# Two more down units prepared in the last up chunk's chain, and half of the final sums added one unit earlier

## The reference

```python
def conv_ffn(h, w_up, conv_w, conv_b, w_down):          # D=2048, FFN_DIM=5632
    u = causal_dwconv(h @ w_up, conv_w, conv_b)          # width 3
    g, val = jnp.split(u, 2, axis=-1)
    return (jax.nn.silu(g) * val) @ w_down

# first block (attention and state-space mixers come before this)
    h = rms_norm(x, norm_ffn_g[l]) * (1.0 + scale_f) + shift_f
    x = x + gate_f * conv_ffn(h, w_up[l], conv_ffn_w[l], conv_ffn_b[l], w_down[l])
return rms_norm(x, final_norm_g)
# second block (RWKV and pooling mixers), with its own weights: the same form
# shift, scale, gate = silu(c) @ w_ada + b_ada, six vectors of 2048 a block
```

## Time and profile before

| | us |
|---|---|
| median of 3 runs | 2575.4 |
| runs | 2571.93, 2575.4, 2576.75 |
| profiled execution, own time | 2577.9 |
| its span, first to last instruction | 2576.2 |
| PE busy | 2395.2 (93%) |
| DVE busy | 1948.6 (76%) |
| ACT busy | 1176.8 (46%) |
| DMA | 615.76 MB, mean 239 GB/s |
| granted TensorE clock, mean | 0.967 |

### The profile page before, as it was taken

One profiled execution on the slowest core, in us unless ns is written; L12 is line 12 of the kernel. 1 busy time (PEld: TensorE's weight loads), 2 busy tenths in 40 slices (PEclk: granted clock), 3 DMA queues, 4 the chain that ended last, 5 costly groups with the idle time before them and its releaser, 6 DMA issues.

```text
span 2576.2 us, 42584 instructions
## 1 busy us (share of the span) xinstructions
PE 2395.2 (93%) x17274; PEld 2148.4 (83%) x17274; DVE 1948.6 (76%) x2310; ACT 1176.8 (46%) x1290; POOL 96.1 (4%) x184
## 2 busy tenths in 40 slices
PE   4899958899999999999899889999899999999997
PEld 4899838888888888887699788889788888888886
DVE  6988878888797788878788576668888655566655
ACT  3344364355553345543444344434565543455442
POOL 0020000000000000000000000000000000000000
PEclk8999979999999999999999999889999999999999
DMA  8988956767777887768578122218576545555552
GB/s 358 421 332 323 341 182 252 303 259 279 280 298 298 330 304 275 272 260 341 189 270 318 67 89 97 95 58 305 227 279 258 187 172 193 183 185 190 180 213 97
DMA packets 88529, 615.76 MB, mean 239 GB/s; under 512 B 9656, under 2 KB 13264, under 8 KB 14928
## 3 DMA queue, kind: packets, MB, share of 16 engines
q1 hardware_dynamic: 65216, 445.07, 46.4%
q0 software_dynamic: 23184, 168.83, 17.5%
HBM read 609.64 MB, written 4.22 MB: 238 GB/s over the span
## 4 chain that ended last, share of the span: by engine, by line
PE 72%; DVE 15%; DMA 5%; ACT 5%; issue 2%; SPq 0%; DVEq 0%; POOLq 0%; ACTq 0%
PE ps L750 35%; PE ps L752 18%; PE ps L745 4%; PE ps L746 4%; PE ps L747 4%; DMA ada_raw<-in_ada_stream 2%; DVE w_lo L1660 2%; DVE ada_raw L1672 2%; DVE first_raw L1672 2%; DMA w_raw<-in_w_stream 1%; ACT w_hi L1128 1%; DMA first_raw<-in_ada_stream 1%; DVE w_lo L1656 1%; PE ps L631 1%; DVE conv_y L1981 1%
## 5 line engine op out<-in xcount | busy, mean ns | idle before, releaser
L750 PE MATMUL ps<-h_both,w_hi 128*128 128x512 f32 x2816 | 991.2, 396 | 15.3 <-DVE h_both L1703 14.4
L752 PE MATMUL ps<-h_both,w_lo 128*128 128x256 f32 x2816 | 791.9, 281 | 0.0
L750 PEld LDWEIGHTS ps<-h_both,w_hi 128*128 128x128 f32 x2816 | 530.4, 188 | 141.9 <-issue 16.7
L1656 DVE TENSOR_TENSOR w_lo<-w_raw,w_hi 128x2048 fp32r<-128x2048 f32 x225 | 513.6, 2287 | 98.9 <-ACT w_hi L1122 98.6
L1122 ACT CAST w_hi<-w_raw 128x2048 fp32r<-128x2048 f32 x226 | 430.6, 1911 | 256.3 <-DMA w_raw<-in_w_stream 243.3
L745 PE MATMUL ps<-h_both,w_hi 128*128 128x256 f32 x1664 | 485.8, 292 | 60.4 <-DVE h_both L1801 33.1
L752 PEld LDWEIGHTS ps<-h_both,w_lo 128*128 128x128 f32 x2816 | 534.6, 190 | 0.0
L750 PE MATMUL ps<-hid_both,w_hi 128*128 128x512 f32 x1344 | 472.6, 394 | 15.2 <-DVE w_lo L1660 15.2
L746 PE MATMUL ps<-h_both,w_hi 128*128 128x256 f32 x1664 | 477.1, 287 | 0.0
L747 PE MATMUL ps<-h_both,w_lo 128*128 128x256 f32 x1664 | 476.5, 286 | 0.0
L1660 DVE TENSOR_TENSOR w_lo<-w_raw,w_hi 128x2048 fp32r<-128x2048 f32 x147 | 335.4, 2288 | 130.8 <-ACT w_hi L1128 130.3
(11 more groups left out here) (355 smaller groups left out, 1823.6 us busy)
## 6 DMA issues: line engine op xcount, KB each, us to landing
w_raw<-in_w_stream SPq DMA_DIRECT2D x372, 1024.0 KB, 4.9
ada_raw<-in_ada_stream POOLq DMA_DIRECT2D x160, 1024.0 KB, 6.9
first_raw<-in_ada_stream SPq DMA_DIRECT2D x32, 1024.0 KB, 10.1
kept_raw<-in_w_stream SPq DMA_DIRECT2D x4, 1024.0 KB, 9.5
x<-in_x_t SPq DMA_DIRECT2D x1, 2048.0 KB, 10.0
cs_b<-cs_rows SPq DMA_DIRECT2D x4, 512.0 KB, 8.1
x_kept<-x SPq DMA_DIRECT2D x1, 2048.0 KB, 13.5
out_t<-x SPq DMA_DIRECT2D x4, 512.0 KB, 2.6
```

Source lines behind the costliest of these rows:

```text
L750: mm(ps[:, b, :].rearrange("p (a t) -> p a t", a=2), hi, both[:, :, k], start=first, stop=False, skip_group_check=True)
L752: return mm(ps[:, b, T:512], lo, big[:, k], start=False, stop=False, skip_group_check=True)
L1656: tt(w_lo[:, slot], w_raw[:, slot], w_hi[:, slot].bitcast(F32), ALU.subtract).then_inc(lo_ready, 1)
```

## The change

It has two parts, and moves that follow from them.

First, units 2 and 3 of each down stage are prepared within the chain of the last up chunk, on ACT (`up_end`) and on DVE (`finish`), and both `down` loops start at q = 4. The ada products that stood at q = 2 and 3 move to later units: in d = 0 to q = 11 and 14, in d = 1 the three of q = 2 and 3 (one and two) go to q = 9, 12 and 13.

Second, in the named stages the kept units are multiplied with `three` into the large half alone. The small half is complete one unit earlier, after unit n-3; PE signals it bank by bank, and DVE adds it while PE starts on the kept units, which wait for it (`down_half`). Behind each kept bank one addition is left where there were two. `lo_unit(u_next)` moves behind the eight small additions, `lo_unit(u_next + 1)` behind the last addition.

```diff
 (PE, down)
+                        if name is not None and q == n - 3 and k < 7:
+                            last.then_inc(S(name + "_small"), 1)
...
                 if name is not None:
-                    pairs = [weights(n - 2), weights(n - 1)]
-                    for b in banks:
-                        for q, (w_h, w_l) in enumerate(pairs):
-                            last = tile(b, w_h, w_l, 2 * (per - 2 + q), False)
+                    kept = [weights(n - 2), weights(n - 1)]
+                    for k, b in enumerate(banks):
+                        pe.wait_ge(down_half, 16 * d + 8 + k + 1)
+                        for q, (w_h, w_l) in enumerate(kept):
+                            for f in range(2):
+                                w, j = slice(f * 1024 + b * P, f * 1024 + b * P + P), 2 * (per - 2 + q) + f
+                                last = three(bank(b), w_h[:, w], w_l[:, w], hid_hi[:, j], hid_lo[:, j], False, False,
+                                             skip_group_check=True)
                         last.then_inc(down_tile, 1)
 (ACT)
+            def up_end(c, par_, ev, u_next):
+                hi_unit(u_next)
+                hi_unit(u_next + 1)
+                ev[0](c, par_)
+                hi_unit(u_next + 2)
+                ev[1](c, par_)
+                hi_unit(u_next + 3)
+                ev[2](c, par_)
+                ev[3](c, par_)
...
-                for q in range(2, n if name is None else n - 4):
+                for q in range(4, n if name is None else n - 4):
                     hi_unit(u0 + q)
 (DVE)
+            def finish(c, e0, evac, u_next):
+                par_ = (e0 + c) % 2
+                lo_unit(u_next)
+                lo_unit(u_next + 1)
+                evac[0](c, par_)
+                lo_unit(u_next + 2)
+                evac[1](c, par_)
+                evac[2](c, par_)
+                lo_unit(u_next + 3)
+                evac[3](c, par_)
...
-                for q in range(2, n - 2 if name is not None else n):
+                for q in range(4, n - 2 if name is not None else n):
...
                 if name is None:
                     lo(0, 0, u_next)
...
+                    for k in range(8, 16, 2):
+                        down_add(d, gate0, k, banks)
+                    lo(0, 1, u_next)
+                else:
+                    for k, b in enumerate(banks):
+                        if k < 7:
+                            dve.wait_ge(S(name + "_small"), k + 1)
+                        else:
+                            dve.wait_ge(units_used, u0 + n)
+                        half_add(gate0, 8 + b, b, T).then_inc(down_half, 1)
+                    if u_next is not None:
+                        lo_unit(u_next)
+                    for k, b in enumerate(banks):
+                        dve.wait_ge(down_tile, 16 * d + 8 + k + 1)
+                        dve.wait_ge(down_half, 16 * d + 8 + k + 1)
+                        half_add(gate0, 8 + b, b, 0).then_inc(down_out, 1)
+                        if k >= 2:
+                            add_square(name, joint, 8 + k - 2)
+                    if u_next is not None:
                         lo_unit(u_next + 1)
...
-            down(0, ..., {**{q: 1 for q in range(2, 11)}, **{q: 1 for q in range(15, 24)}}, UP1B, U_UP1B)
+            down(0, ..., {q: 1 for q in range(4, 24) if q not in (12, 13)}, UP1B, U_UP1B)
-            down(1, ..., {2: 1, 3: 2, 4: 1, 5: 1, 6: 1, 7: 1, 8: 1, 14: 1, 15: 1, 16: 1, 17: 1}, C_LORA, U_LORA,
+            down(1, ..., {4: 1, 5: 1, 6: 1, 7: 1, 8: 1, 9: 1, 12: 1, 13: 1, 14: 1, 15: 1, 16: 1, 17: 1}, C_LORA, U_LORA,
                  "mid", 2)
```

More of the change, by code:

```diff
@@ L1160, in up_body, with stream @@
                 return body
-            def stream(u0, e0, c0, c1, evac, u_next, ahead=True):
+            def up_end(c, par_, ev, u_next):
[7 more added lines that the diff above has]
+                ev[3](c, par_)
+            def stream(u0, e0, c0, c1, evac, u_next):
                 hi(c0, 2, u0)
@@ L1167, in stream @@
                 chunk_runs(act, c0 + 1, c1, e0, up_body(u0, evac))
[L1168 to L1174, removed]
+                up_end(c1 - 1, (e0 + c1 - 1) % 2, evac, u_next)
             def none(c, par_):
@@ L1396, in _ @@
             chunk_runs(act, 9, 12, UP1A, up_body(U_UP1A, ev))
[L1397 to L1400, removed]
+            up_end(11, (UP1A + 11) % 2, ev, U_DN1A)
             down(0, U_DN1A, 2 * FFN_A, UP1B, U_UP1B)
@@ L1710, in gains_of, with stream @@
                 return [gain[:, k:k + 1] for k in range(KT)]
[L1712 to L1722, removed]
+            def finish(c, e0, evac, u_next):
[8 more added lines that the diff above has]
+                evac[3](c, par_)
+            def stream(u0, e0, c0, c1, evac, p0, pairs, u_next=None):
                 def some_ada(c, i, odd):
@@ L1759, in stream @@
                 if u_next is not None:
-                    finish(c1 - 1, e0, evac, u_next, ahead)
+                    finish(c1 - 1, e0, evac, u_next)
             def plain_body(u0, evac):
@@ L1997, in hidden, with half_add @@
                 return (add, taps, product, rest)
+            def half_add(gate0, j, b, t0):
+                return stt(out=x[:, j], in0=ps[:, b, t0:t0 + T], scalar=mod[:, gate0 + j:gate0 + j + 1], in1=x[:, j], op0=ALU.mult,
+                           op1=ALU.add)
             def down_add(d, gate0, k, banks):
@@ L2001, in down_add @@
                     dve.wait_ge(down_tile, 16 * d + e + 1)
[L2002 to L2005, removed]
+                    half_add(gate0, 8 * (e // 8) + banks[e % 8], banks[e % 8], 0).then_inc(down_half, 1)
                 for e in (k, k + 1):
                     dve.wait_ge(down_half, 16 * d + e + 1)
[L2008 to L2011, removed]
+                    half_add(gate0, 8 * (e // 8) + banks[e % 8], banks[e % 8], T).then_inc(down_out, 1)
             def add_square(name, n, k):
@@ L2042, in down @@
                     lo(0, 0, u_next)
[L2043 to L2046, removed]
-                        lo_unit(u_next + 1)
[L2048 to L2054, removed]
+                    for k in range(8, 16, 2):
[17 more added lines that the diff above has]
+                    if u_next is not None:
+                        lo_unit(u_next + 1)
                 dve.wait_ge(down_out, 16 * d + 16)
@@ L2091, in _ @@
             mod_bias(GATE_F, KT)
-            down(0, U_DN1A, 2 * FFN_A, GATE_F, 104, {**{q: 1 for q in range(2, 11)}, **{q: 1 for q in range(15, 24)}}, UP1B, U_UP1B)
+            down(0, U_DN1A, 2 * FFN_A, GATE_F, 104, {q: 1 for q in range(4, 24) if q not in (12, 13)}, UP1B, U_UP1B)
             stream(U_UP1B, UP1B, 0, FFN_B, hidden(UP1B, FFN_A, "fcw"), 122, 2, U_DN1B)
@@ L2095, in _ @@
             steps.link(tt(gain[:], gain[:], pcol("final_g", 0, KT), ALU.mult))
-            down(1, U_DN1B, 2 * FFN_B, GATE_F, 142, {2: 1, 3: 2, 4: 1, 5: 1, 6: 1, 7: 1, 8: 1, 14: 1, 15: 1, 16: 1, 17: 1}, C_LORA, U_LORA,
+            down(1, U_DN1B, 2 * FFN_B, GATE_F, 142, {4: 1, 5: 1, 6: 1, 7: 1, 8: 1, 9: 1, 12: 1, 13: 1, 14: 1, 15: 1, 16: 1, 17: 1}, C_LORA, U_LORA,
                  "mid", 2)
```

## The result

The changed kernel took 2547.2 us (median of 4 runs, 2538.43 to 2555.16), the kernel before beside it 2573.7 (4 runs, 2570.94 to 2576.75). The ratio is 0.9896 with a 95% interval of 0.9861 to 0.9931: 26.5 us less. The forecast was 2549 and 26.8 less. Two more comparisons of the same two kernels, told under "The up chunks", gave 23.7 and 21.2 us less between the medians.

The account below looks back on a forecast made before the run. PE's waits for other engines were taken as the bound (72% of the chain on PE). 19.1 + 2.5 - 1.0 - 0.9 + 5.9 + 1.2 = 26.8 us less, from 2575.4 to about 2549, range 2543 to 2559.

Parts of the forecast that it names:

- Units 2 and 3 in the chain: Openings of the four down stages: preparing both units inside the last up chunk's chain removes the stall, gaining 19.1 us.
- rival (b): Openings and tails: the clock is not returned, only waits go; 18.3 us gained, 2557; chance 0.10.
- (c): Down stage openings: the stall moves to unit 4, whose DMA waits for unit 0; 8 to 12 gained, 2565; chance 0.05.
- The clock behind the stall: Down stage openings: slow stretch returned with each removed wait, 1.7 us (d=0), nearly 3 (d=2), hardly any (d=3).
- The rest of d = 1: Loss in d=1 beyond its opening, where DVE waits for ada rows: 2.5 us gained, bounds 0 and 3.6.
- The moved ada products: Later units of d=0 and d=1: the added DVE work costs 1.0 us, bounds 0 and 5.
- Rival (a): DVE becomes the bound inside the down stages as moved ada products meet a late row: 20.3 gained, 2555; chance 0.16.
- Three for wide: Kept units of d=1 and d=3: triples cost 0.360 us against 0.3467 for the wide pair, 0.9 in all.
- The added waits: Kept units: PE's wait on `down_half` and DVE's small additions cost nothing unless DVE is over 4 us late.
- rival (e): Kept units: DVE reaches the small additions late and PE waits there, nothing gained, 2575; chance 0.03.
- (d): Down stages slower: loads average 11.5 us, each of 30 ada units 1.4 late; 42 lost, 2590; chance 0.02.
- The tails: Ends of d=1 and d=3: 5.9 us gained in d=1 (4.1 wait, 1.8 six matmuls), 1.2 in d=3.

Follow-up runs that it names:

- unit2_only: The changed kernel with unit 3 prepared behind the last chunk's chain again, only unit 2 in it: 2547.9 us in one run (before 2573.1).
- split_only: The kernel before with only the second part of the change (early small half, kept units with `three`, moved `lo_unit`): 2565.7 us, ratio 0.9965.
- lo_late: The kernel before with only `lo_unit(u_next + 1)` moved behind the last addition of d=1: 2571.7 us in one run (before 2573.1).
- d1_single: The kernel before with one of the two ada products of q=3 moved to q=9 in d=1: 2579.3 us in one run (before 2573.1).
- spread12: The changed kernel; in d=1 two ada products (units 12, 13) moved into the second block, unit 9's moved to unit 12: 2551.0 us, ratio 0.9911.
- after_again: The changed kernel once more, with no edit: 2549.3 us (4 runs), ratio 0.9901.
- after_third: The changed kernel a third time, with no edit: 2549.5 us (6 runs), ratio 0.9911.
- chain_only: The kernel before with only the first part of the change (openings and moved ada products), stage ends as before: 2557.6 us, ratio 0.9928.

## Why the prediction was right, and where it was off

**Units 2 and 3 in the chain**: right. 4.9, 6.0 and 3.2 came where 4.9, 6.0 and 3.3 stood, and the price had been read off the stages' length, not off the list of waits. The four waits (12.4) would have told two thirds of it. The clock came back with them, so rival (b) is out. Unit 4 was not late, so (c) is out. That unit 3 is part of the step was not needed (`unit2_only`).

**The clock behind the stall**: the size per stage was taken for a property of the stage, "1.7 in d = 0, nearly 3 in d = 2, hardly any in d = 3". It is not. Four kernels here have the stalled openings (before, `split_only`, `lo_late`, `d1_single`), 16 in all. From the first matmul of the stage to the start of unit 2, the wait included, it was always 14.3 to 14.4 us, 3.3 more than the 11.1 without a stall. Unit 2 itself took 5.63 in three of them (one in d = 1, two in d = 3), 7.2 in eleven and 8.3 in two (one in d = 2, one in d = 0), against 5.55: 0.1, 1.65 or 2.7 more. The mean is 1.5, so a stalled opening costs 4.8 on average, four of them 19.0. That the prediction's 19.1 agrees is partly the fortune of one trace.

**The rest of d = 1**: 2.5 was too little; all 3.6 came back. Units 3, 5 and 7, which end where PE waits for units 4, 6 and 8, went from 6.94, 6.09 and 6.91 to 5.55 each, and in `d1_single`, with a single product less in unit 3, they took 5.55 too. But 3.6 too is the figure of one trace: `lo_late`, with the same products, lost 1.7 there and `split_only` 4.6.

**The moved ada products**: -1.0 was too little; they cost 3.0 in the trace of after and 2.1 in each of its repeats, all of it in d = 1. Rival (a) named units 12 and 13 of d = 0, which have no wait, and 11, 16 and 17 of d = 1, which do. It came true in part, within the bounds of 0 and 5 and beside the full return of the other term, which (a) had ruled out. DVE in d = 1 of the changed kernel: the first sums and the wait at unit 12, then what stands ahead of unit 17, and PE's first matmul of unit 17:

```profile
1201.72 6.35 DVE L2009 SCALAR_TENSOR_TENSOR x<-ps,mod,x 128x256 f32<-128x256 f32 x16
...
1211.67 2.29 DVE L1667 TENSOR_TENSOR w_lo<-w_raw,w_hi 128x2048 fp32r<-128x2048 f32 x1 [1.40 <-ACT w_hi L1134]
...
1239.14 2.29 DVE L1679 SCALAR_TENSOR_TENSOR ada_raw<-ada_raw,ada_c 128x2048 f32<-128x2048 f32 x1 [0.51 <-DMA ada_raw<-in_ada_stream]
...
1241.36 2.29 DVE L2028 TENSOR_TENSOR kept_lo<-kept_raw,kept_hi 128x2048 fp32r<-128x2048 f32 x1
1243.56 2.29 DVE L1667 TENSOR_TENSOR w_lo<-w_raw,w_hi 128x2048 fp32r<-128x2048 f32 x1
1245.99 0.47 PE L750 MATMUL ps<-hid_both,w_hi 128*128 128x512 f32 x1 [1.44 <-DVE w_lo L1667]
```

What was wrong is the slack, "between 1.1 and nothing". It rested on sums that end 7.3 to 8.5 after unit 9's start, as in the kernel before (7.55). But the product added at unit 9 stands ahead of them, and here they ended at 9.41 (unit 9 starts at 1198.66). It also took DVE's 36 us of work as free of gaps, and DVE stood still 1.40 for the rounding of unit 12, whose load took 10.7. In the kernel before it stood still 1.93 at the same place, with two products less to do behind it. Last, the row of one product came 0.51 late. Counted from 8.4, the end of the sums that leaves no slack, that makes 1.0 + 1.4 + 0.5 = 2.9, and unit 17 started 47.3 after unit 9, 2.9 behind the 44.4. That the product at unit 9 moved the sums shows in `spread12`, which lacks it there: they ended at 8.65, though DVE waited about 1.0 for a row ahead of them as in the changed kernel. The late row, which rival (a) is built on, is the smallest of the three and not needed: in `after_again` and `after_third` no row was late between the sums and unit 17, the sums ended at 9.75 and 9.51, DVE stood still 0.77 and 1.00 at unit 12, and unit 17 was 2.0 late.

In the sum the errors of the two terms, +1.1 and -2.0, leave 0.9 too much.

**Three for wide**: -0.9 was too much. The changed kernel's kept matmuls, start, us:

```profile
1252.33 0.28 PE L745 MATMUL ps<-hid_both,kept_hi 128*128 128x256 f32 x1
...
1253.38 0.28 PE L745 MATMUL ps<-hid_both,kept_hi 128*128 128x256 f32 x1
```

Between them lie nine matmuls, 1.05 us, so 0.1167 each and 0.350 a triple, against 0.3467 for the wide pair: 3 ns a triple and 0.1 us a stage. d = 3 took 110.9 with `three` and 110.8 without (`chain_only`). The prediction's 0.360 came from a stretch in another part of the kernel. The Trainium skill's page "TensorE: Matmul & The Clock Gate", section "Back-to-back issue gap", had it closer: its constant gives 2.5 ns for one instruction more. Here the measurement of that difference is on the side of the rule. It is not for the gap itself: by the rule one of 256 columns takes 109.2 ns, an estimate, and 116.7 was measured. The row was the wrong one to take, since its matmuls run at 120 ns each and those of a down stage at 116.7.

**The added waits**: nothing, as predicted. PE's list for the whole of d = 1 has one row, and none for the additions of the small half, so rival (e) is out:

```profile
PE ps L750 <- DVE w_lo L1667: 2.3, 3, 1.4
```

The weight loads took 7.1 in the median in d = 0 and 6.7 in d = 1, not 11.5, and PE in d = 0 waits nowhere: (d) is out. "Loads over 10" had been named as a sign of being wrong; one load of a streamed unit was over, the 10.7 of unit 12.

**The tails**: 4.2 and 1.7 for 4.1 and 1.8, and 1.3 for 1.2. Right in each number, and the bound of 0 for the clock did not come in.

**How much of it was luck**: the mechanism held, term by term, for the openings and the tails. That the total came within 0.3 did not follow from it. The errors of the three other terms, +1.1, -2.0 and +0.7 for the split, nearly cancel, the opening's price and the 3.6 were single draws, and the repeats of the comparison gave 23.7 and 21.2.

## What to carry to other kernels

Price a stall by the length of its stage against the stage at rest, not by the wait alone, and take the slow stretch behind it from several openings, since one trace draws it. When work is moved off one stall, recount the engine that gets it instruction by instruction, in its new order and with the idle times that the old trace shows; the three products that cost 2 to 3 us here stood where the count had left 1.1 to nothing, and it had missed 1.0 of shift and 1.4 of idle time. A cost per instruction is read from the stage in which it will run.

## What the hardware showed that was not expected

**Two rhythms of the same matmuls.** In the up chunks the pair of a 512-column and a 256-column matmul takes 347 ns or 353 ns. In the faster one three pairs take 1040 ns, in the slower 1060. The windows under "The up chunks" show both: 579 matmuls in 100 us, and 567 to 569. The change from one to the other, in the timeline of before:

```profile
556.09 0.28 PE L752 MATMUL ps<-h_both,w_lo 128*128 128x256 f32 x1
556.32 0.50 PE L750 MATMUL ps<-h_both,w_hi 128*128 128x512 f32 x1
556.66 0.28 PE L752 MATMUL ps<-h_both,w_lo 128*128 128x256 f32 x1
556.77 0.40 PE L750 MATMUL ps<-h_both,w_hi 128*128 128x512 f32 x1
```

The starts at 556.32 and 556.66 come late (230 ns behind the start before, where 117 are usual, and 340, where 230 are). Ahead of them the gaps repeat as 120, 235, 114, 232, 118, 241, behind them as 117, 230.

In 13 traces of 11 different kernels, 52 stages in all, nine ran in the faster rhythm from their third chunk on or earlier, two changed in their last third (one to each side), and the others stayed in the slower; the first block's stage B never ran in the faster one. A late start is neither needed nor enough: in `after_third` the rhythm changed with all starts within 5 ns of their usual gaps, and in the trace of after a hiccup like the one above, at 529.02, changed nothing. The down stages, with the same shapes, ran at 5.547 a unit in every trace. The granted clock reads 1.00 in both rhythms. What sets them stays open: neither the shift of 256 bytes nor the order of the tiles does, and nothing else was tried. The three stages that were ever seen in the faster rhythm are worth 5.0, 5.0 and 4.2 us, and no trace had all three; that is of the size of the spread between runs of one kernel, which was not taken apart further.
